# Two packed inverses in an RWKV-7 mixer: the order of their doubling levels

## The reference, cut to what matters

```
S = (S * w_t - einsum('bhvk,bhk->bhv', S, kk_t)[..., None] * (kk_t * a_t)
     + v_t[..., None] * k_t)
o_t = einsum('bhvk,bhk->bhv', S, r_t)
```

```
y = (o - mu) * rsqrt(var + GN_EPS) * gn_w + gn_b + bonus;  y * (sigmoid(glo) @ g_up)
```

## Time and profile before

| | us |
|---|---|
| Median of 3 executions | 3133.6 (3133.14, 3133.6, 3151.87) |
| The profiled execution | 3133.81 |
| Its span (first to last instruction) | 3132.0 |
| Around the span (3133.81 - 3132.0) | 1.8 |
| Mean granted TensorE clock | 0.975 of full speed |
| The eight mixer passes, 749.5 to 1204.0 | 454.5 |
| One pass in the middle | 57.7 to 57.8 |

### The profile page before, as it was taken

One profiled execution on the slowest core, in us unless ns is written; L12 is line 12 of the kernel. 1 busy time (PEld: TensorE's weight loads), 2 busy tenths in 40 slices (PEclk: granted clock), 3 DMA queues, 4 the chain that ended last, 5 costly groups with the idle time before them and its releaser, 6 DMA issues.

```text
span 3132.0 us, 52077 instructions
## 1 busy us (share of the span) xinstructions
PE 2950.7 (94%) x21870; PEld 2420.1 (77%) x21870; DVE 2135.2 (68%) x2657; ACT 1274.0 (41%) x1578; POOL 377.5 (12%) x534
## 2 busy tenths in 40 slices
PE   4899999877998998999999999999889999999999
PEld 2588987635777776888888888899757888888887
DVE  3587776567777875578878888669955655555554
ACT  2322222165555553344444444456443433434342
POOL 1000000002354341012122121000000000000000
PEclk8799999988999998999999999999989999999999
DMA  9986887793000033678888888655335555565553
GB/s 328 350 292 221 307 310 263 254 350 113 23 13 15 23 70 135 191 269 296 285 292 298 293 294 298 206 182 179 122 94 175 190 191 187 192 192 189 192 178 131
DMA packets 306023, 640.73 MB, mean 205 GB/s; under 512 B 19035, under 2 KB 23937, under 8 KB 303585
## 3 DMA queue, kind: packets, MB, share of 16 engines
q1 hardware_dynamic: 269280, 529.94, 50.2%
q0 software_dynamic: 28384, 94.76, 9.2%
q10 hardware_dynamic: 8128, 12.72, 1.1%
HBM read 623.81 MB, written 13.40 MB: 203 GB/s over the span
## 4 chain that ended last, share of the span: by engine, by line
PE 85%; DVE 7%; DMA 4%; ACT 2%; issue 2%; ACTq 0%; SPq 0%; DVEq 0%
PE ps L467 46%; PE ps L506 15%; PE ps L508 8%; DMA raw<-in_ada_w_dram 3%; PE ps L486 2%; PE ps L1807 1%; PE ps L2613 1%; PE ps L1955 1%; PE ps L404 1%; PE ps L1907 1%; DVE rw_mt L1489 1%; DVE rw_mb L1487 1%; DVE rw_scc L1470 1%; PE ps L3165 1%; PE ps L1691 1%
## 5 line engine op out<-in xcount | busy, mean ns | idle before, releaser
L444 DVE TENSOR_TENSOR split_lo<-raw,split_hi 128x2048 fp32r<-128x2048 f32 (+1 forms) x372 | 849.3, 2286 | 468.2 <-ACT split_hi L432 460.3
L432 ACT ACTIVATE split_hi<-raw 128x2048 fp32r<-128x2048 f32 x368 | 702.1, 1913 | 1082.4 <-PE ps L467 750.0
L506 PE MATMUL ps<-xa,split_hi 128*128 128x512 f32 x2048 | 721.0, 397 | 4.2 <-ACT xa L665 4.2
L508 PE MATMUL ps<-xa,split_lo 128*128 128x256 f32 x2048 | 573.0, 280 | 0.0
L506 PEld LDWEIGHTS ps<-xa,split_hi 128*128 128x128 f32 x2048 | 385.1, 188 | 98.0 <-ACT xa L665 4.5
L467 PE MATMUL ps<-split_hi,hT_hi 128*128 128x512 f32 x992 | 387.1, 390 | 0.0
L508 PEld LDWEIGHTS ps<-xa,split_lo 128*128 128x128 f32 x2048 | 386.8, 189 | 0.2
L467 PE MATMUL ps<-split_hi,hT_lo 128*128 128x512 f32 x992 | 386.0, 389 | 0.0
L467 PE MATMUL ps<-split_lo,hT_hi 128*128 128x512 f32 x992 | 386.0, 389 | 0.0
L467 PEld LDWEIGHTS ps<-split_hi,hT_hi 128*128 128x128 f32 x992 | 186.2, 188 | 40.2 <-issue 1.8
L467 PEld LDWEIGHTS ps<-split_hi,hT_lo 128*128 128x128 f32 x992 | 186.2, 188 | 39.0
(11 more groups left out here) (436 smaller groups left out, 4600.6 us busy)
## 6 DMA issues: line engine op xcount, KB each, us to landing
raw<-in_mlp_w_dram SPq DMA_DIRECT2D x256, 1024.0 KB, 5.6
raw<-in_ada_w_dram SPq DMA_DIRECT2D x64, 1024.0 KB, 9.0
raw<-in_mix_in_w_dram SPq DMA_DIRECT2D x48, 1024.0 KB, 5.9
raw<-in_conv_pw_w_dram SPq DMA_DIRECT2D x48, 1024.0 KB, 5.3
gate<-in_ada_w_dram SPq DMA_DIRECT2D x172, 256.0 KB, 4.9
line<-in_ada_w_dram POOLq DMA_DIRECT2D x171, 256.0 KB, 5.0
late<-in_ada_w_dram POOLq DMA_DIRECT2D x85, 256.0 KB, 5.0
tmpa<-in_ada_w_dram SPq DMA_DIRECT2D x84, 256.0 KB, 4.8
```

The costliest lines, as they stand in the source:

```text
L432: nc.scalar.activation(split_hi[:, c, :, 0:n], raw[:, c, :, 0:n], ACT.Copy).then_inc(hi_done, 1)
L444: nc.vector.tensor_tensor(split_lo[:, c, :, 0:n], raw[:, c, :, 0:n], split_hi[:, c, :, 0:n], ALU.subtract).then_inc(lo_done, 1)
L506: pe.matmul(ps[:, base + j, :], split_hi[:, c, kk, j * P:(j + 1) * P], both, start=(k == 0), stop=False, skip_group_check=True)
L508: mm = pe.matmul(ps[:, base + j, 0:SEQ], split_lo[:, c, kk, j * P:(j + 1) * P], xa_hi[:, k, :], start=False, stop=(k == KT - 1), skip_grou ...
```

## The change

The order of the twelve steps is written as a list, `LEVEL_ORDER`. Tile 0 runs one level ahead of tile 1: 0, 2, 1, 4, 3, 6, 5, 8, 7, 10, 9, 11. No instruction is added or taken away; the semaphore counts of the waits follow the new order through small functions that look up a step's place in the list. Beside the order of the steps themselves:

- PE: `opened` 0 goes ahead of the scores of the last chunk, `update` 0 right behind these, and the variance behind `update` 0. `corners` are split: the first behind update 1, the second behind update 4. `opened_corner` stands behind updates 3 and 5, `gates` behind update 6, `bonus` still behind update 8.
- DVE: `chunk_decays` and `bonus_values` stand ahead of the last transposes (k = 11) instead of behind them.
- ACT: the copy of step 2 goes ahead of late scores 6 and 7 and of `deviation`; the copies of the corners stand behind steps 3 and 6, `gate_values` behind step 8.

```diff
+        LEVEL_ORDER = [0, 2, 1, 4, 3, 6, 5, 8, 7, 10, 9, 11]
+        z_no = lambda k: LEVEL_ORDER.index(k) + 1
+        mt_no = lambda k: [j for j in LEVEL_ORDER if j < NT_DVE].index(k) + 1
+        mb_no = lambda k: [j for j in LEVEL_ORDER if j >= 2].index(k) + 1
+        zz_no = lambda k: k + 1 if k < 2 else 2 + mb_no(k)
...
@@ ACT, inverse @@
-                corners(x, 0)
-                corners(x, 1)
-                for k in range(NT_DVE):
-                    level_values(x, k)
-                    if k == 3 and not first:
+                for k in LEVEL_ORDER[1:]:
+                    if k >= 2:
+                        level_values(x, k - 2)
+                    if k == 2:
+                        late_scores(x, range(6, 8))
+                        if not first:
+                            deviation(x.last())
+                    elif k == 3:
+                        corners(x, 0)
+                    elif k == 6:
+                        corners(x, 1)
+                    elif k == 8 and not first:
                         gate_values(x.last())
...
@@ ACT, body @@
                 packed(x, 1)
-                late_scores(x, range(6, 8))
-                if not first:
-                    deviation(x.last())
                 inverse(x, first)
...
@@ DVE, inverse @@
                 masked(x, 0)
                 mask_scores(x, 3)
-                for k in range(NS):
-                    if k:
-                        masked(x, k)
-                chunk_decays(x)
-                bonus_values(x)
+                for k in LEVEL_ORDER[1:]:
+                    if k == NS - 1:
+                        chunk_decays(x)
+                        bonus_values(x)
+                    masked(x, k)
...
@@ PE, inverse @@
-                for c in range(4):
+                for c in range(3):
                     scores(x, c, first)
                     if c == 1 and not first:
                         mean(x.last())
+                opened(x, 0)
+                scores(x, 3, first)
+                update(x, 0)
                 if not first:
                     variance(x.last())
-                opened(x, 0)
-                update(x, 0)
-                corners(x, 0)
-                corners(x, 1)
                 opened(x, 1)
-                for k in range(1, NS):
+                for k in LEVEL_ORDER[1:]:
                     if k < NT_DVE:
                         update(x, k)
-                    if k in (2, 3):
-                        opened_corner(x, k - 2)
-                    if k == 1 and not first:
+                    else:
+                        last_update(x, k)
+                    if k == 1:
+                        corners(x, 0)
+                    elif k == 4:
+                        corners(x, 1)
+                    elif k in (3, 5):
+                        opened_corner(x, k // 2 - 1)
+                    elif k == 6 and not first:
                         gates(x.last())
                     elif k == 8:
                         bonus(x, first)
-                last_update(x, NS - 2)
-                last_update(x, NS - 1)
                 corner_half(x, 0)
                 corner_turn(x, 0)
                 corner_half(x, 1)
```

More of the change, by code:

```diff
@@ L1185, in level_values @@
             def level_values(x, k):
-                act.wait_ge(W["mb"], x.n(NT_DVE, k + 1))
+                act.wait_ge(W["mb"], x.n(NT_DVE, mb_no(k + 2)))
                 nc.scalar.activation(rw["zz"][:, k % 2, :, :], ps[:, ZB[k % 2], :].rearrange("p (j s) -> p j s", s=HB), ACT.Copy).then_inc(W["zz"], 1)
             def own_blocks(x, b):
-                act.wait_ge(W["z_lev"], x.n(NS, NS - 1 + b))
+                act.wait_ge(W["z_lev"], x.n(NS, z_no(NS - 2 + b)))
                 h = own_half(0)
@@ L1485, in masked @@
                 else:
-                    dve.wait_ge(W["z_lev"], x.n(NS, k - 1))
+                    dve.wait_ge(W["z_lev"], x.n(NS, z_no(k - 2)))
                     V.tensor_tensor(out, ps[:, ZB[b], :].rearrange("p (d j s) -> p d j s", d=2, s=HB), m, ALU.mult).then_inc(W["mb"], 1)
-                    dve.wait_ge(W["mb"], x.n(NT_DVE, k - 1))
+                    dve.wait_ge(W["mb"], x.n(NT_DVE, mb_no(k)))
                 V.transpose(rw["mt"][:, b, :, :].rearrange("p j s -> p (j s)"), rw["mb"][:, b, :, :].rearrange("p j s -> p (j s)")).then_inc(W["mt_d"], 1)
             def last_blocks(x, k, b):
-                dve.wait_ge(W["z_lev"], x.n(NS, k - 1))
+                dve.wait_ge(W["z_lev"], x.n(NS, z_no(k - 2)))
                 for d in range(2):
@@ L1505, in own_blocks @@
                 steps.wait()
-                dve.wait_ge(W["z_lev"], x.n(NS, NS - 1 + b))
+                dve.wait_ge(W["z_lev"], x.n(NS, z_no(NS - 2 + b)))
                 h = own_half(1)
@@ L1787, in last_update @@
                 b = k % 2
-                pe.wait_ge(W["mb"], x.n(NT_DVE, k - 1))
-                pe.wait_ge(W["zz"], x.n(NS + 2, k + 1))
+                pe.wait_ge(W["mb"], x.n(NT_DVE, mb_no(k)))
+                pe.wait_ge(W["zz"], x.n(NS + 2, zz_no(k)))
                 for j in range(4):
@@ L1802, in update @@
                 b = k % 2
-                pe.wait_ge(W["mt_d"], x.n(NT_DVE, k + 1))
-                pe.wait_ge(W["zz"], x.n(NS + 2, k + 1))
+                pe.wait_ge(W["mt_d"], x.n(NT_DVE, mt_no(k)))
+                pe.wait_ge(W["zz"], x.n(NS + 2, zz_no(k)))
                 for j in range(8):
```

## The result

The changed kernel is slower: 3159.67 us median (3151.63 to 3163.5, 11 runs) against 3142.17 us for the kernel before in runs beside it (3126.69 to 3151.87, 11 runs). The ratio is **1.0054, 95% interval 1.0036 to 1.0073**. I had forecast 3132 with a range of 3122 to 3142: that the change stays within 1% held, the sign and the range did not. The three runs that stood ahead of the prediction were not typical either: over more runs the kernel before has its median at 3138 to 3142, and 3133.6 lies in its lower part. One execution of the kernel before, among those beside runs 9 to 12, took 3751.47 us at a mean granted clock of 0.738 and is left out.

A forecast was written before the change was run, and what follows sets the result against it. The prediction took each mixer pass as bound by a chain from PE to DVE to ACT and back, without transfer waits. Eight passes gaining 0.2 us each took 1.6 from 3133.8, giving 3132 us, range 3122 to 3142.

The forecast's parts named there:

- The bound by stages: Mixer passes: a middle pass of 57.7 us waits for no transfer, being a chain from PE to DVE to ACT and back.
- the replay: New queues replayed on one middle pass's clock: 0.2 us gained per pass, 3132 us, own range 3129 to 3135, chance 0.50.
- step (1): First opening product ahead of the last scores: these and tile 1's packing come 0.3 us late, or 0.15 with weights loaded beforehand.
- The gap of the gates: DVE's wait while the gate products hold PE: moved behind update 6, not removed, giving back 0.9 us ahead of step 7's mask.
- PE's idle piece: Tail of a pass, ahead of the last small update: PE idle about 2.1 us in one piece.
- step (2): Update 0 right behind the scores, so DVE masks step 2 in its first gap: lead 0.3 us.
- step (3): Start of the levels: DVE's second gap shrinks to 0.3 us and the third goes: lead 2.0 us.
- steps (4) to (7): Gates, bonus and tile 1 alone at the end spend the lead; the pass finally gains 0.1 to 0.35 us.
- The case that the change does not do what it says: Rival: ACT's copies behind a table load come late for step 4; passes 0.8 us longer, 3140 us; chance 0.08.
- rival A: Granted clock falls in the tail where PE idles: 3138 us with falls in half the passes, 3144 in all; chance 0.30.
- priced a fall: Half clock behind a pass's tail: 3 to 4 us of it cost 1.2 to 1.7 us of pass.
- 8 x 0.2 = 1.6: Gain over all eight mixer passes, 0.2 us each, the first pass counted like the others.

The follow-up runs named there:

- runs 9 to 12: Gates version with idle products everywhere, 3134.9 us; changed kernel with three idle products, 3128.19; kernel before unchanged, 3154.36; kernel before with early opening and idle products, 3129.23.
- run 4: Changed kernel with the bonus product behind step 6 and the gate products behind update 9, in the tail's idle time: 3127.95 us median, ratio 0.9968.
- run 8: Changed kernel ending 9, 10, 11, chunk decays and bonus values ahead of 9, bonus behind 6, gates behind 7, five idle products in first pass: 3137.69 us.
- run 11: The kernel before, unchanged, in one more profiled execution: 3154.36 us.
- run 2: Kernel before with seven idle products in the three short gaps of its tail: 3129.53 us median, ratio 0.9977.
- run 1: Changed kernel with eight idle products on PE between update 9 and the last small update: 3130.67 us median, ratio 0.998.
- run 10: Changed kernel with three idle products behind update 9: 3128.19 us median, ratio 0.9967.
- run 5: Kernel before with only the last three steps exchanged to 10, 9, 11 on every engine: 3169.35 us median, ratio 1.0079.
- run 6: Kernel before with only the first opening product ahead of the last scores, update 0 behind them, then the variance: 3142.4 us median, ratio 1.0027.
- run 3: Changed kernel with the steps in the old order 0 to 11 and all its other moves kept: 3168.77 us median, ratio 1.0107.

## Why the prediction was wrong

**What held.** The bound by stages and the replay held in the main. A pass at full clock takes 57.70 to 57.71 against 57.77; I had said 0.2 less, between 0.1 and 0.35, and it is 0.07. The upper end was added up wrongly: with the second copy ending at 892.85 against 892.90 and a delay in step (1) that can be 0.15 smaller, the replay's own bounds are 0.05 and 0.20, and 0.07 lies in them. The gap of the gates moved from step 4 to step 7 at 0.90 for 0.9; ahead of step 9 DVE waited 0.26 for my 0.4, ahead of the last transposes 0.53 for 0.4; PE's idle piece is 2.17 for my 2.1. Counted from the end of tile 0's packing, the delay of step (1) is 0.22, the lead of step (2) 0.2 for my 0.3, and that of step (3) 2.3 for my 2.0; steps (4) to (7) spend it: the gates and the bonus product where they now stand, and tile 1 alone at the end. Runs 4 and 8 win 0.9 us of a pass with the gates moved out of DVE's way. The case that the change does not do what it says was wrong: ACT kept up.

**What failed.** The choice between the replay and rival A: the sum of 3132 has no term for the granted clock in the tail, and that clock fell in five of the seven passes and in the last one. I had the mechanism, its place and its sign, and gave it 0.30 against 0.50. I weighed the tail before ("PE was busy for 1.32 of 3.50 us and the clock stayed at 1.00") as evidence that short idle pieces are harmless. That was luck of one execution: run 11 shows a fall behind that very tail, and run 2 suggests that part of the spread of the kernel before comes of it. With such a tail near the edge, a piece twice as long deserved the larger chance.

**The mis-sized terms.** Even with A the sum would have ended at 3138 to 3144. I priced a fall at 1.2 to 1.7 us, from 3 to 4 us at half clock. My two rows give 1.1 to 1.4 for that; the 1.71 us in them was not at half clock from its start, for the fall came at 1193.9, and eight such products wholly at half clock take 1.97. The price by length was near: 3.4 us at half clock cost 1.0 us in run 8. What was off is the length. The clock stayed at half for 6.8 to 10.2 us: the last four passes grew by 3.8 each (61.48 - 57.70), the first by 2.9 (59.59 - 56.67, run 1), together 18.0 of the 18.2 that the seven passes lost. The last pass, which I had priced like the others, lost 9.1, with 27.3 us at half clock; against run 1, where nothing fell in it, it lost 13.3. I take it that its stay was so long because its scan has no work of a next pass beside it, but that is not shown: PE was busy for 25.4 of these 27.3 us, and passes with such work had stays of 34 us, which cost 15.0 (run 11).

The gain was mis-sized too: for 8 x 0.2 = 1.6 us the seven passes without falls show a loss of 0.2 (402.9 against 402.7, runs 1 and 10). Six passes win 0.05 to 0.07 each and the first, which I had counted with the others, loses 0.55.

**The baseline.** I took 3133.8 as the sum's foot, from three runs of which the third, 3151.87, was a warning that I passed over. Applied to that foot the measured ratio gives 3150.7, still outside the range: the baseline is not the reason of the miss.

**What is shown, and what is left open.** Shown: filling the idle piece removes the falls with all else equal (runs 1, 10, in the profile of each, and by a median 29 us and more below the changed kernel's, against 4 us at most between the medians of before beside them), and the tail of the new order adds them to the kernel before (run 5), where two idle pieces grow at once. Not shown: why the second and third pass of the changed kernel had the same piece and no fall (run 8 says that where a pass lies in time has a share); whether and why the early opening alone makes falls more frequent (run 6); why the clock stays at half for 3.4 us in one pass and 34 in another. The stages ahead of and behind the mixer also vary between executions of unchanged code (the part behind the start of the projection took 1908.3 to 1922.0); I did not trace that further.

## What to carry to other kernels

Before reordering PE's queue around a chain of waits, look for the longest piece in which PE would stand idle; here a piece of 2 us cost more than the whole reorder could win, and it cost in the scan behind it, where PE was busy nearly all the time (9.5 of 10.2 us). Put work that has slack (here the gate products) into such a piece, and judge an order by the pass length at full clock and by the granted clock apart, because their sum in one run hides both. The falls depend on more than the order, so compare them over several executions. Where three runs differ by more than the expected gain, take that spread as part of the mechanism to explain.

## What the runs showed of the hardware that I had not expected

- Passes with a fall repeated at nearly the same length in three kernels whose passes differ: 61.45 to 61.50 in the last four of the changed kernel, 61.44 to 61.46 in the last five of run 5, 61.46 to 61.53 in the last four of run 3. Without falls the changed kernel's pass is 57.70. Once it has fallen, a loop of this length seems to stay in step with the next fall; no run here isolates that.
- Passes with the same work and the same idle pieces fell for 3.4, 6.8 and 0 us in turn (run 8).
- Useless products on PE can be worth their time: three of them per pass (0.9 us of PE) took the changed kernel from 3159.67 us (beside 3142.17 for before) to 3128.19 (beside 3141.25).
- A stay at half clock can last ten times as long as another (3.4 us in run 8, 34.1 us in runs 6 and 11), though PE was busy for 33.5 of 34.1 us in it (run 11). In the changed kernel 10.2 us at half clock cost 3.8 us of a pass.
